# Output and gate projections of a hybrid decoder step in 2x2 blocks with seven products

## What is computed

```python
def mixer_layer(x, ple, ..., lp):
    h = rmsnorm(x, lp['norm_g'])
    proj = h @ lp['w_in']
    ...                      # gated DeltaNet, RWKV-7 and block-sparse attention: o_a, o_b, o_c
    o = jnp.stack([o_a, o_b, o_c], axis=2)
    up = jnp.einsum('blnc,ncd->blnd', o, lp['w_branch'])
    gates = jax.nn.sigmoid(gate_raw + lp['b_gate']).reshape(B, L, N_BRANCH, D_MODEL)
    x = x + jnp.sum(gates * up, axis=2) @ lp['w_out']
    x = x + jax.nn.sigmoid(x @ lp['w_pg'] + lp['b_pg']) * (ple @ lp['w_ple'])
```

## Time and profile before

| | |
|---|---|
| median of three runs | 1173.02 us (1172.61 to 1175.12) |
| the profiled execution | 1172.17 us, span 1170.4 us from its first to its last instruction |
| TensorE (PE) busy | 1134.9 us, 97% of the span, 8148 MATMUL records |
| weight loads (PEld) busy | 862.5 us, beside the matmuls |
| VectorE (DVE), ScalarE (ACT), GpSimd (POOL) busy | 572.7, 329.2, 131.9 us |
| transfers | 148.45 MB, mean 127 GB/s |
| mean granted TensorE clock | 0.995 |
| stages of layer 0: `p_up(2)`, `p_y`, `p_pg` with `p_ple` | 504.2 to 519.7, to 550.8, to 590.2 us |
| the same of layer 1 | 1076.9 to 1092.4, to 1123.5, to 1164.4 us |

### The profile page before, as it was taken

The page is one execution under the profiler, slowest core; times in us unless marked ns, Lnnn a source line. Parts: engine busy times, 40 slices in busy tenths (PEclk is TensorE's granted clock), DMA queues, the critical chain, the costliest instruction groups (busy, mean ns, idle before and its releaser), DMA issues. The chain is left out here.

```text
span 1170.4 us, 20948 instructions
## 1 busy us (share of the span) xinstructions
PE 1134.9 (97%) x8148; PEld 862.5 (74%) x8148; DVE 572.7 (49%) x1267; ACT 329.2 (28%) x722; POOL 131.9 (11%) x215
## 2 busy tenths in 40 slices
PE   8999999999999899999999999999999998999998
PEld 6778777767777577777767778777777776777776
DVE  3477546776765304221236774666667633161212
ACT  2233222322343153300123422233234232423001
POOL 0121402020101000000001123211102011000000
PEclk9999999999999899999999999999999999999999
DMA  6742146422413945364237321643223077443621
GB/s 218 209 151 85 50 135 205 103 65 75 91 38 84 288 150 179 91 208 152 74 111 213 108 79 56 195 149 90 74 57 92 19 203 239 151 132 108 221 81 41
DMA packets 168655, 148.45 MB, mean 127 GB/s; under 512 B 41705, under 2 KB 157007, under 8 KB 168365
## 3 DMA queue, kind: packets, MB, share of 16 engines
q1 hardware_dynamic: 164167, 136.65, 39.9%
q0 software_dynamic: 2848, 7.79, 2.0%
q10 hardware_dynamic: 1541, 2.66, 0.7%
HBM read 135.42 MB, written 11.07 MB: 125 GB/s over the span
## 5 line engine op out<-in xcount | busy, mean ns | idle before, releaser
L1137 PE MATMUL psum<-x_a,ring 128*128 128x288 f32 x1296 | 338.1, 411 | 0.5 <-DVE x_a L2244 0.5
L1137 PE MATMUL psum<-x_b,ring 128*128 128x288 f32 x1296 | 338.5, 412 | 0.0
L1137 PEld LDWEIGHTS psum<-x_b,ring 128*128 128x128 f32 x1296 | 240.1, 191 | 69.0 <-issue 7.7
L1137 PEld LDWEIGHTS psum<-x_a,ring 128*128 128x128 f32 x1296 | 239.5, 191 | 68.9 <-issue 8.4
L1784 ACT ACTIVATE arena<-psum 128x512 f32<-128x512 f32 (+5 forms) x150 | 67.3, 472 | 164.6 <-PE psum L1062 101.2
L1137 PE MATMUL psum<-z,ring 128*128 128x288 f32 x384 | 98.0, 409 | 0.0
L1137 PEld LDWEIGHTS psum<-z,ring 128*128 128x128 f32 x384 | 71.4, 190 | 20.6 <-issue 2.3
L1784 ACT ACTIVATE arena<-arena 128x256 f32<-128x256 f32 (+9 forms) x102 | 44.5, 464 | 65.1 <-DVE arena L2830 28.1
L1062 PE MATMUL psum<-consts,arena 128*128 128x128 f32 (+2 forms) x362 | 53.9, 283 | 8.9 <-DMA arena<-in_x_prompt 4.6
L1137 PE MATMUL psum<-merged,ring 128*128 128x288 f32 x256 | 62.4, 406 | 0.0
L1062 PEld LDWEIGHTS psum<-consts,arena 128*128 128x128 f32 (+2 forms) x362 | 43.4, 147 | 23.1 <-issue 7.3
(11 more groups left out here) (404 smaller groups left out, 1419.9 us busy)
## 6 DMA issues: line engine op xcount, KB each, us to landing
ring<-in_w_in SPq DMA_DIRECT2D x72, 1024.0 KB, 5.3
ring<-in_w_branch SPq DMA_DIRECT2D x24, 512.0 KB, 3.7
arena<-in_cache_k SPq DMA_DIRECT2D x32, 256.0 KB, 3.1
arena<-in_cache_v SPq DMA_DIRECT2D x32, 256.0 KB, 3.1
ring<-in_w_out SPq DMA_DIRECT2D x8, 1024.0 KB, 7.2
ring<-in_w_pg SPq DMA_DIRECT2D x8, 1024.0 KB, 5.2
arena<-in_state_dn SPq DMA_DIRECT2D x8, 512.0 KB, 7.4
out_dn_sample<-arena POOLq DMA_DIRECT2D x8, 512.0 KB, 6.3
```

Of the source, the lines that this page charges most:

```text
L1137: ins = mm(out[:, 0:NTOK], lhs, rhs(k), **flags)
```

## The change

The output channels of `w_out` and `w_pg` are taken in pairs of blocks (q = 0..3), the input blocks in pairs j, and the tokens in two halves of 144. In place of eight products of a 2x2 block scheme (two output blocks, two input blocks, two token halves) there are seven, numbered 1 to 7, each a chain over j = 0..3 with 144 columns:

- 1: W(0,0) with the first half; 2: W(1,0) with the first half, added to 1 in bank 0; 3 to 7 with sums of weights or of token halves; 1 is copied by ScalarE (`seed`) from bank 0 to bank 1 or 7, where 6, 7 and 4 are added to it one after the other; 5 and 3 use bank 2.
- The weight sums (two new tiles and two made in place, each 128 x 4 x 128) are made on GpSimd, three of them a pair ahead, the fourth when product 1 has read its weights.
- The token differences (four per j) are made on VectorE: those of the merged branches during `p_up(2)`, those of x after product 3 of each `w_y` pair.
- In `w_y` VectorE adds the PSUM banks to x in half-width pieces (six per pair, `plus`); in `w_pg` ScalarE and VectorE collect the banks in SBUF and `x_out` finishes a block. In `w_y` and `w_pg`, 4 and 3 of a pair come after product 1 of the next pair.
- All eight `p_ple(m)` move ahead, the first right behind `p_up(2, 7)`, and are copied to SBUF by ScalarE. The transfer of their weights is emitted at `p_up(2, 0)` in place of `p_up(2, 4)`.
- `w_branch` chunks hold four m and 1 MB. Banks of the other projections are chosen by which was read longest ago. `Y_ENDS` has four ends. `norm` of layer 1 squares the last block.
- `FILL` is a new list. For instance it puts 1 and 28 pieces before `c_rope(0)` and `c_rope(1)` in place of 10 and 14, and 543 in place of 546 up to and with the second; 40 stay ahead of `a_rows`.

```diff
-Y_ENDS = {3: 0, 6: 4, 7: 7}
+Y_ENDS = {3: 0, 5: 4, 7: 7, 6: 6}
+HALF = NTOK // 2
...
-    "ple_w_loaded": {"p_up": (16, lambda st: st[2:] == (2, 4))},
+    "ple_w_loaded": {"p_up": (16, lambda st: st[2:] == (2, 0))},
+    "ple_read": {"p_ple": (1, None)},
+    "sums": {"p_up": (1, lambda st: st[2] == 2 and st[3] in (4, 5, 6)), "w_y": (1, lambda st: st[-1] in (1, 6, 2, 5)),
+             "w_pg": (1, lambda st: st[-1] == 1 or st[-1] in (6, 2, 5) and st[2] < 3)},
...
+def bank_of(q, i):
+
+    return 0 if i in (1, 2) else 2 if i in (5, 3) else 1 if q % 2 else 7
...
+        add("p_ple", 0)
+
+        def products(kind, q, *numbers):
+            for i in numbers:
+                add("half", kind, q, i)
+                add(kind, q, i)
+
+        behind = None
+        for kind, q in [("w_y", q) for q in range(4)] + [("w_pg", q) for q in range(4)]:
+            if (kind, q) == ("w_pg", 0) and l + 1 < DEPTH:
+                order.append(("params_t", l + 1))
+            products(kind, q, 1)
+            add("seed", kind, q)
+            if (kind, q) == ("w_y", 0):
+                add("p_ple", 1)
+            if behind:
+                products(*behind, 4, 3)
+            if (kind, q) == ("w_pg", 0):
+                add("p_ple", 2)
+                add("p_ple", 3)
+            products(kind, q, 6)
+            if kind == "w_pg" and q:
+                add("x_out", 2 * q - 2)
+            products(kind, q, 2)
+            if kind == "w_pg" and q:
+                add("x_out", 2 * q - 1)
+            products(kind, q, 5, 7)
+            if (kind, q) == ("w_pg", 0):
+                for m in range(4, 8):
+                    add("p_ple", m)
+            elif kind == "w_pg" and l + 1 == DEPTH:
+                add("y_out", 2 * q - 2)
+                add("y_out", 2 * q - 1)
+            behind = (kind, q)
+        products("w_pg", 3, 4, 3)
+        add("x_out", 7)
+        add("x_out", 6)
...
-            a = 256 * (m // 2)
-            tile(i, (kind, l, n, m // 2), w_br[l, n, :, :, a:a + 256], 4, 128 * (m % 2), 256)
-        elif kind in ("p_y", "p_pg"):
-            a = 256 * (m // 2)
-            tile(i, (kind, l, m // 2), (w_out if kind == "p_y" else w_pg)[l, :, :, a:a + 256], KT_,
-                 128 * (m % 2), 256)
+            a = 512 * (m // 4)
+            tile(i, (kind, l, n, m // 4), w_br[l, n, :, :, a:a + 512], 4, 128 * (m % 4), 512)
...
+            def multiply(kind, l, m, js):
+
+                p, i = (kind, l) + m[:-1], m[-1]
+                n = pair_no[p]
+                c, w = weights(p)
+                b = bank_of(*m[-2:])
+                if js[0] == 0:
+                    if i == 1:
+                        pe.wait_ge(S.sem(f"ring{c % RING}_loaded"), 16 * (c // RING + 1))
+                    pe.wait_ge(S.sem(f"bank{b}_read"), S.count(f"bank{b}_read", S.at - 1))
+                    if i == 6:
+                        pe.wait_ge(S.sem("bank0_read"), S.count("bank0_read"))
+                        if p[2] == 0:
+                            pe.wait_ge(S.sem("ple_read"), S.count("ple_read", pos[("p_ple", l, 0)]))
+                    if i in (5, 6, 7):
+                        made = ("p_up", l, 2, {5: 4, 6: 5, 7: 6}[i]) if p[0] == "w_y" and p[2] == 0 else pair_steps[n - 1] + ({5: 6, 6: 2, 7: 5}[i],)
+                        pe.wait_ge(S.sem("sums"), S.count("sums", pos[made]))
+                    elif i == 3:
+                        pe.wait_ge(S.sem("sums"), S.count("sums", pos[p + (1,)]))
+                src = operand(kind, l)
+                for j in js:
+                    if p[2] == 0:
+                        operands_ready(kind, l, i, j)
+                    lhs = (w[:, j, 0, 0], w[:, j, 1, 0], w[:, j, 0, 0], w[:, j, 1, 1], weight_sum(n, 1)[:, j], weight_sum(n, 2)[:, j], w[:, j, 0, 1])[i - 1]
+                    rhs = (half_tokens(src, 0, 0), half_tokens(src, 1, 0), half_tokens(src, 1, 1), token_sum(kind, l, 4), token_sum(kind, l, 1),
+                           token_sum(kind, l, 2), token_sum(kind, l, 3))[i - 1][:, j]
+                    ins = mm(PS[:, b, 0:HALF], lhs, rhs, start=i in (1, 5) and j == 0, stop=j == 3, skip_group_check=True)
+                return ins
...
+            def seed(l, kind, q):
+                b = bank_of(q, 6)
+                act.wait_ge(S.sem("projected"), S.count("projected", pos[(kind, l, q, 1)]))
+                act.wait_ge(S.sem(f"bank{b}_read"), S.count(f"bank{b}_read"))
+                if q == 0:
+                    act.wait_ge(S.sem("ple_read"), S.count("ple_read", pos[("p_ple", l, 0)]))
+                fn(PS[:, b, 0:HALF], PS[:, 0, 0:HALF], ACT.Copy).then_inc(S.sem("bank0_read"), 1)
...
+            def square(l, n):
+                act.wait_ge(S.sem("x_next"), S.count("x_next", pos[("x_out", l, OUT_ORDER[n])]))
+                fn(SQX[:, n % 2, :], H(l)[:, OUT_ORDER[n], :], ACT.Square).then_inc(S.sem("squares"), 1)
...
+            def x_out(l, m):
+                n = OUT_ORDER.index(m)
+                act.wait_ge(S.sem("bank2_read"), S.count("bank2_read", pos[("w_pg", l, m // 2, (3, 7)[m % 2])]))
+                gate_tanh(m, 1, TG[:, m // 2 % 2, m % 2, HALVES[1]], "z_tanh")
                 if l + 1 == DEPTH:
                     return
...
+                if n:
+                    square(l, n - 1)
+                if n == 7:
                     logs()
-                act.wait_ge(S.sem("x_next"), S.count("x_next"))
-                act.wait_ge(S.sem("squares"), S.count("squares", S.at - 1))
-                fn(TMP[:, 2, :], H(l)[:, m, :], ACT.Square).then_inc(S.sem("squares"), 1 if m < 7 else 2)
-                act.wait_ge(S.sem("squares"), S.count("squares") - (m < 7))
 
             def norm(l):
-                logs()
+                if l:
+                    square(l - 1, 7)
+                else:
+                    logs()
...
-                if (n, m) == (2, 4):
-
+                if (n, m) == (2, 0):
...
+                if n == 2 and m % 2:
+                    for i in range(4):
+                        difference("w_y", l, m // 2, i + 1).then_inc(S.sem("h_ready"), 1)
+                        if i in (0, 1):
+                            dve.wait_ge(S.sem("h_ready"), S.count("h_ready") - 3 + i)
+
+            def difference(kind, l, j, i):
+
+                src = operand(kind, l)
+                b11, b12, b21, b22 = (half_tokens(src, x, h)[:, j] for x in range(2) for h in range(2))
+                of, less = ((b12, b11), (b22, token_sum(kind, l, 1)[:, j]), (b22, b12), (b21, token_sum(kind, l, 2)[:, j]))[i - 1]
+                return tt(token_sum(kind, l, i)[:, j], of, less, SUB)
...
+                if i == 6:
+                    plus(2 * q, 1, b)
+                elif i == 2:
+                    plus(2 * q, 0, 0)
+                elif i == 7:
+                    plus(2 * q + 1, 1, b)
+                    plus(2 * q + 1, 1, 2)
+                elif i == 4:
+                    plus(2 * q + 1, 0, b)
+                elif i == 3:
+                    plus(2 * q, 1, 2)
+                    for t in range(4):
+                        difference("w_pg", l, q, t + 1).then_inc(S.sem("h_ready"), 1)
+                        if t in (0, 1):
+                            dve.wait_ge(S.sem("h_ready"), S.count("h_ready") - 3 + t)
...
+            def x_out(l, m):
+                dve.wait_ge(S.sem("z_tanh"), S.count("z_tanh"))
+                i = (2, 4)[m % 2]
+                b = bank_of(m // 2, i)
+                dve.wait_ge(S.sem(f"bank{b}_read"), S.count(f"bank{b}_read", pos[("w_pg", l, m // 2, i)]))
+                dve.wait_ge(S.sem("ple_read"), S.count("ple_read", pos[("p_ple", l, m)]))
+                link(stt(TMP[:, m % 2, :], TG[:, m // 2 % 2, m % 2, :], 1.0, PLO[:, m, :], ADD, MUL))
+                tt(H(l)[:, m, :], TMP[:, m % 2, :], X(l)[:, m, :], ADD).then_inc(S.sem("x_next"), 1)
+                if l + 1 < DEPTH and m:
                     dve.wait_ge(S.sem("squares"), S.count("squares") - 1)
-                    ins = tt(TMP[:, 3, :], TMP[:, 3, :], TMP[:, 2, :], ADD) if m else cp(TMP[:, 3, :], TMP[:, 2, :])
+                    square = SQX[:, (OUT_ORDER.index(m) - 1) % 2, :]
+                    ins = tt(TMP[:, 3, :], TMP[:, 3, :], square, ADD) if m > 1 else cp(TMP[:, 3, :], square)
                     ins.then_inc(S.sem("squares"), 1)
...
+            def sums_ahead(n, i):
+
+                c, w = weights(pair_steps[n])
+                if i == 1:
+                    pool.wait_ge(S.sem(f"ring{c % RING}_loaded"), 16 * (c // RING + 1))
+                dst, one, two, op = ((weight_sum(n, 1), w[:, :, 0, 1], w[:, :, 1, 1], ADD), (weight_sum(n, 2), weight_sum(n, 1), w[:, :, 0, 0], SUB),
+                                     (w[:, :, 0, 1], w[:, :, 0, 0], w[:, :, 0, 1], SUB))[i - 1]
+                tt(dst, one, two, op).then_inc(S.sem("sums"), 1)
+
+            def p_up(l, n, m):
+                if n == 2 and m in (4, 5, 6):
+                    if m == 4:
```

(63 more changed lines are left out.)

195 lines of the change are left out of this document (114 added, 81 removed), and 12 rows, old and new, of the table FILL.

## The result

The changed kernel takes 1176.84 us (median of 14 runs, 1173.62 to 1180.19), the kernel before 1172.8 us beside it (14 runs, 1169.84 to 1175.12): ratio 1.0038, 95% interval 1.0027 to 1.0048. I had forecast 1167.0 with a range up to 1175.0. It is slower by 4 us where I expected 6 us less. The profiled execution took 1176.86 us, its span is 1174.6 us against 1170.4.

What follows compares the result with a forecast made beforehand. The prediction took TensorE, busy 97% of the span, as the bound. Its terms, -14.4 + 11.3 + 3.7 - 11.9 + 2.5 + 1.7 + 1.1, summed to -6.0 us, giving 1167.0 us from 1173.02, range 1156.5 to 1175.

Steps and rivals of the forecast that it cites:

- products: p_y and p_pg on TensorE: 448 half-width records at 122.5 ns, 54.9 us a layer for 62.1; -14.4 us.
- port between VectorE and GpSimd: In w_y and w_pg, VectorE's SBUF-only work and GpSimd's weight sums block each other, so TensorE waits; +11.3 us (0 to +16).
- weights of `p_ple`: At p_ple(0) of layer 0, TensorE waits 1.7 to 4.0 us for weights issued behind params_load; +3.7 us.
- `c_rope`, chunks: At c_rope, fewer ring loads ahead land the swap earlier: idle time -8.4 us, half-clock work -3.5, together -11.9.
- layer boundary, with clock: Between the last product and the next layer's first: more serial work, +2.5 us, and a lowered clock, +1.7.
- end: After the last product, serial VectorE work delays the first store of y to 2.8 us from 1.66; +1.1 us.
- rest of FILL: Elsewhere the new list moves pieces by a few between steps showing no long wait; 0, +-1.5 us.
- the rival on weight loads: In the half-width products, weight loads at 190 ns set the pace: +30 us a layer, 1227 us; chance 2%.
- The stall per pair: In pairs 1 to 3 of w_y, product 7 waits 1.45 us for product 6's eviction; +8.7 us over two layers.
- the rival with no stall: In w_y and w_pg, differences and sums fall between each other, costing TensorE nothing: 1156.5 us; chance 16%.
- The rival in which the swap's own transfer sets the wait at `c_rope`: The wait at c_rope stays: +2.9 us in place of -11.9, 1181.8 us at most; chance 8%.
- Rival (e): The change does as forecast, but the old order's 0.5 to 0.8 us waits elsewhere grow: +3, 1170 us; 12%.

Runs made afterwards that it cites:

- a_oldfill: The changed kernel with the old FILL list, all else as changed; 1169.89 us, ratio 0.9984 to the kernel before.
- o_nosums: The changed kernel with the old FILL, GpSimd's weight sums cut to 4 of 512 elements, products 5 and 6 reading plain weights; 1158.75 us, ratio 0.9894.
- b_chunks: The kernel before with only p_up's weight chunks changed, 1 MB for four column blocks in place of 512 KB for two; 1160.59 us, ratio 0.9894.
- a_ple_defer: The changed kernel, new FILL, with the w_ple transfer issued ahead of params_load and token differences moved behind the next pair's evictions; 1167.28 us, ratio 0.9949.
- a_shift: The changed kernel with 128 waits on a long-reached semaphore added to TensorE's queue at the layer boundary; 1180.44 us, ratio 1.0065.
- o_defer: The changed kernel with the old FILL and w_y's token differences moved behind evictions of the next pair, except the last pair's; 1162.62 us, ratio 0.9918.
- a_noload: The changed kernel with two ring loads of layer 1 cut from 128 partitions to one, computing with old weights there; 1170.82 us, ratio 0.9989.
- b_chunks_fill: The kernel before with the 1 MB chunks for p_up and the new FILL, old products; 1173.03 us, ratio 1.0.

## Why the prediction was wrong, step by step

The trace after minus the trace before, by the terms of the sum (spans, +4.2 us in all):

| term | forecast | measured | how |
|---|---|---|---|
| products | -14.4 | -14.4 | 448 records a layer at 122.5 ns from start to start |
| port between VectorE and GpSimd | +11.3 | +10.1 | six stalls of 1.21 us and 0.16 us of drain, +8.2; in `w_pg` 0.52, 0.51 and 0.38 with drain, +1.9 |
| weights of `p_ple` | +3.7 | +4.5 | 2.66 us with drain, and 1.7 us by the clock |
| `c_rope`, chunks | -11.9 | -11.1 | waits 9.55 to 1.93 us; no half clock behind them, -3.5 |
| layer boundary, with clock | +4.2 | +3.8 | last product to first one 4.4 us before, 8.2 now |
| end | +1.1 | +0.8 | last product to the end of the span 6.0 us before, 6.8 now |
| rest of FILL | 0 | +10.5 | what is left of the +4.2; 8.0 of it ahead of `p_up(2)`, both layers together |

**The step that failed** is one sentence: "The rest of FILL moves pieces by a few between steps that show no long wait: 0, +-1.5." The new list changed when TensorE's code had to come and which loads were then under way, and that cost was put at nothing. Stage by stage, the time outside the edited stages and `c_rope` grew by 8.0 us:

- 5.3 us, all in layer 1, are the two waits for code (2.20 and 1.37 us) with the half clock behind the first (1.7).
- 1.3 us are there by 27 us already, where the traces differ among themselves (the 100th matmul record stands between 22.5 and 27.3 us in all of them), and are no effect of the change that these runs can show.
- 1.4 us are left for the rest of the mixers. Some of their small waits grew: those of the block inverses (L1430 and L1447, beside the waits for code) by 1.7 us in all, those of the `b_norm` steps on L2973 (0.67 to 1.16) and L2991 (none to 0.45). Others went: the 0.79 us that a `b_norm` step cost on L2971 in each layer (L2788 before), so that `b_norm` as a whole waits only 0.1 us more a layer.

The other 2.5 us of the row do not belong to FILL. They lie in the edited stages, as a term that the prediction left out: it named the blocks of y turned back between products of layer 1 (L1150) only as cover. They take 3.5 us of TensorE where they took 2.0, since TensorE waits twice for `x_out` there:

```profile
1149.47 0.55 PE L1150 MATMUL psum<-consts,x_a 128*128 128x128 f32 x3 [0.31 <-DVE x_a L2476]
```

The last 1.0 us I can't place. The runs with the list alone point the same way, +7 and +12 us by the medians; these hold what the list costs at `c_rope` as well (waits of 1.9 us for 0.2 in `a_oldfill`, 4.4 for 0.8).

Why I missed it: I read the waits of the kernel before and took a place without a wait as a place with slack, but a wait of zero says nothing of the margin. And neither the waits nor the groups show when code arrives; only the queue of the kind "instruction" does, and I had not read it. Before, that queue had 66 transfers, none of which left TensorE waiting for as much as 0.5 us.

**Steps that held.** The pace of 144-column records is 122.5 ns, so the rival on weight loads (1227) falls. The Trainium skill's page "TensorE: Matmul & The Clock Gate", section Back-to-back issue gap, by whose rate I estimated 79 us for a layer's products, doesn't agree: they take 54.9. The stall per pair was forecast at 1.45 us and is 1.37; the rival with no stall (1156.5) falls by `o_nosums`. The rival in which the swap's own transfer sets the wait at `c_rope` falls by `b_chunks`. Rival (e), small waits that grow with the new FILL, priced at 3 us, came true for 1.4 us at most; the waits for code, 5.3 us, stood in no rival. The line between the two rows of 128 and 288 columns gives 124.2 ns at 144, not the 124.6 of the prediction; nothing hangs on it.

**Sizes that were off.** The clock: I had it fall behind one new idle stretch of about 4 us; it fell behind those of 2.66 and 2.20 us as well. The port: its sum is near the forecast partly by luck, for the 1.8 us put on the last pairs of `w_pg` in layer 0 were 0.5, and the first pair of `w_pg` took 0.7 us a layer where I had 0.4. The products' part was forecast at +5.9 without the chunks and the FILL. From `p_up(2)` to the next layer's first product, or to the end, the traces before and after give +7.4 in both layers together; the medians give +9 with the old FILL and +4 with the new one, each with an uncertainty of 2 to 3 us.

## What to carry to other kernels

Where a list sets the order of the work, as FILL does here, a new list is a change of its own: time it alone on the old code before pricing the rest. Two parts of one change that pull by 12 us each way look like no change, and one of the two best kernels here needs only two lines of the diff. Put instructions that may block on another engine behind the evictions that someone is waiting for, not ahead of them.

## What the runs showed of the hardware

- TensorE can run out of code. In eight such waits of 0.9 us or more, in six of these traces, it resumes 1.2 to 1.5 us after a 16 KB code transfer ends, and the transfer starts in the last 0.7 us of a load's packets; each cost 0.9 to 4.7 us, plus the clock, all in the stages of many 64x64 matmuls. The Trainium skill, page "Runtime: NRT & Kernel Launch", section Instruction fetch mechanics, says that crossing a 16 KB boundary is mostly hidden. In most of the 69 cases of the changed kernel it is; behind a ring load, in that stage, it isn't.
- From 25 us on, the granted clock stayed at 2.4 GHz through every wait of 1.21 and 1.37 us and fell to 1.2 GHz, for 3.4 to 10.2 us, in or behind each of 3.4 us and more. Between, both were seen: it fell behind 2.15 us (`a_oldfill`), 2.20 and 2.66 (the changed kernel), 2.45 (`a_ple_defer`) and 2.92 (`a_shift`, for 6.8 us), and not behind 2.06 (`o_defer`), 2.19 (`a_ple_defer`), 2.58 (`a_noload`) and 2.88 (`b_chunks_fill`). So a wait of 2 to 3 us costs 0 to 3.4 us on top, and which, no length in these runs tells. Nor is one long wait needed: in `b_chunks` and `b_chunks_fill` the clock fell for 3.4 us at the layer boundary (590.1 and 587.5), where the longest wait is 1.14 us and shorter ones stand beside it; before, with the same waits, it didn't.
